# Fewer weight chunks in layer 1 on a shorter row ring, and matmuls that keep TensorE busy at both ends

## What is computed

```python
def peer_ffn(h, w_query, sub_keys, expert_u, expert_v):
...
        q = (xb @ w_query).reshape(PEER_BLOCK, PEER_HEADS, 2, D_HALF)
        s = jnp.einsum('thpd,hpkd->thpk', q.astype(jnp.float32), sub_keys.astype(jnp.float32))
        sv, si = lax.top_k(s, TOPK_HALF)
...
        idx = i1 * N_KEYS + i2
        g = jax.nn.softmax(cv, axis=-1)
        u_sel = expert_u[idx]
        a = jax.nn.gelu(jnp.einsum('thkd,td->thk', u_sel, xb))
        return jnp.einsum('thk,thkd->td', g.astype(a.dtype) * a, expert_v[idx])

def reference(...):
...
    for i in range(DEPTH):
        hp = rms_norm(xp, norm_mix[i])
...
            yp, _ = chunk_mlp_mixer(hp, a_w_in[j], a_ln_g[j], a_ln_b[j], a_w_s[j], a_b_s[j], a_w_out[j])
...
            yp, bp = short_conv_mixer(hp, zero_buf, b_w_in[j], b_conv_w[j], b_w_out[j])
...
        f = peer_ffn(tok, peer_w_query[i], peer_sub_keys[i], peer_expert_u[i], peer_expert_v[i])
```

## Time and profile before

| | |
|---|---|
| median of 3 runs | 1724.96 us (1724.49 to 1726.6) |
| the profiled execution, its own time | 1727.62 us |
| its span, first to last instruction | 1725.8 us |
| mean granted TensorE clock | 0.815 |
| TensorE busy | 1316.3 us (76%) |
| VectorE busy | 1086.5 us (63%) |
| ScalarE busy | 651.7 us (38%) |
| GpSimd busy | 632.7 us (37%) |
| moved by DMA | 709.99 MB, 411 GB/s over the span |
| of it by the gathers' queue (q0) | 608.85 MB |

### The profile page before, as it was taken

The page is one execution under the profiler, slowest core; times in us unless marked ns, Lnnn a source line. Parts: engine busy times, 40 slices in busy tenths (PEclk is TensorE's granted clock), DMA queues, the critical chain, the costliest instruction groups (busy, mean ns, idle before and its releaser), DMA issues.

```text
span 1725.8 us, 23657 instructions
## 1 busy us (share of the span) xinstructions
PE 1316.3 (76%) x8378; PEld 631.5 (37%) x8378; DVE 1086.5 (63%) x2681; ACT 651.7 (38%) x2105; POOL 632.7 (37%) x596
## 2 busy tenths in 40 slices
PE   8998988998975678777754688797897667666744
PEld 7993545644540145433100355352462111111100
DVE  1359578555764756565676755767587666666454
ACT  2125444334433432243443423333643434434343
POOL 2014334433442433233344333434444443344341
PEclk9998999998985799997655799798897666667655
DMA  9989999999999999999999999999999999999997
GB/s 379 403 357 415 398 420 422 420 421 421 411 422 421 421 421 420 421 418 421 419 412 421 402 422 421 421 415 416 397 420 411 422 422 421 421 420 419 419 398 306
DMA packets 99382, 709.99 MB, mean 411 GB/s; under 512 B 11488, under 2 KB 11920, under 8 KB 13600
## 3 DMA queue, kind: packets, MB, share of 16 engines
q0 software_dynamic: 84192, 608.85, 85.4%
q1 hardware_dynamic: 14352, 99.16, 14.0%
q10 hardware_dynamic: 720, 0.48, 0.1%
HBM read 706.92 MB, written 1.52 MB: 410 GB/s over the span
## 4 chain that ended last, share of the span: by engine, by line
DMA 49%; PE 32%; ACT 7%; DVE 7%; issue 3%; POOL 2%; DVEq 0%; ACTq 0%; SPq 0%; POOLq 0%
DMA uvring<-expert_uv_dram,idx 48%; PE psum L841 12%; PE psum L852 11%; DVE uvring L1587 5%; PE psum L905 3%; PE psum L1017 3%; POOL uvring L789 2%; ACT diag L1189 1%; ACT wgt L1185 1%; ACT L1177 1%; ACT a_gelu L1177 1%; PE psum L1039 1%; PE psum L860 1%; PE psum L1000 1%; ACT L1075 1%
## 5 line engine op out<-in xcount | busy, mean ns | idle before, releaser
L1587 DVE SCALAR_TENSOR_TENSOR uvring<-uvring,xn 128x1024 f32<-128x1024 f32 x576 | 705.0, 1225 | 531.0 <-DMA uvring<-expert_uv_dram,idx 525.1
L789 POOL DMA_INDIRECT uvring<-expert_uv_dram,idx x576 | 623.9, 1083 | 1038.7 <-PE psum L841 848.8
L841 PE MATMUL psum<-uvring,diag 64*64 64x512 f32 x4096 | 686.4, 764 | 293.0 <-ACT diag L1189 280.4
L1177 ACT ACTIVATE a_gelu<-a_raw 128x1 f32<-128x1 f32 x576 | 116.6, 202 | 867.2 <-DVE uvring L1587 866.8
L841 PEld LDWEIGHTS psum<-uvring,diag 64*64 64x64 f32 x4096 | 130.7, 154 | 722.9 <-ACT diag L1189 636.6
L1189 ACT ACTIVATE diag<-twin,wgt 128x64 f32<-128x64 f32 x512 | 178.1, 348 | 48.8 <-ACT wgt L1185 1.9
L1185 ACT ACTIVATE wgt<-a_gelu,gate 128x1 f32<-128x1 f32 x576 | 169.5, 294 | 21.1 <-ACT a_gelu L1177 0.4
L833 PE MATMUL psum<-uvring,diag 128*32 128x256 f32 x512 | 67.6, 634 | 94.2 <-ACT diag L1189 83.6
L852 PEld LDWEIGHTS psum<-xT,wring 128*128 128x128 f32 x864 | 118.9, 198 | 42.0 <-issue 41.1
L852 PE MATMUL psum<-xT,wring 128*128 128x160 f32 (+1 forms) x864 | 130.3, 306 | 0.0
L852 PEld LDWEIGHTS psum<-xT,kept 128*128 128x128 f32 x896 | 115.3, 192 | 33.9 <-issue 32.3
(11 more groups left out here) (186 smaller groups left out, 957.3 us busy)
## 6 DMA issues: line engine op xcount, KB each, us to landing
wring<-w_chunks_dram SPq DMA_DIRECT2D x51, 1024.0 KB, 10.1
kept<-w_chunks_dram SPq DMA_DIRECT2D x20, 1024.0 KB, 14.3
uvring<-w_chunks_dram SPq DMA_DIRECT2D x17, 1024.0 KB, 17.3
uvring<-expert_uv_dram,idx POOLq DMA_INDIRECT x576, 13.4
arena<-w_chunks_dram SPq DMA_DIRECT2D x2, 1024.0 KB, 14.4
uvring<-w_chunks_dram SPq DMA_DIRECT2D x2, 512.0 KB, 7.4
uvring<-ln_gain_dram POOLq DMA_DIRECT2D x1, 1024.0 KB, 9.4
uvring<-ln_bias_dram POOLq DMA_DIRECT2D x1, 1024.0 KB, 15.0
```

The costliest lines, as they stand in the source:

```text
L789: pool.indirect_dma_start(uvring[:, n % RING, :], None, expert_uv, bass.IndirectOffsetOnAxis(ap=idx[t][:, i:i + 1], axis=0),).then_inc(uv_ ...
L841: mm = nc.tensor.matmul(acc[64 * j:64 * j + 64, 512 * i:512 * (i + 1)], diag[64 * i:64 * i + 64, n % DIAGS, :], row[64 * i:64 * i + 64, D ...
L1177: nc.scalar.activation(a_gelu[:, c:c + 1], a_raw[:, c:c + 1], ACT.Gelu_apprx_tanh).then_inc(gelu_done, 1)
L1587: nc.vector.scalar_tensor_tensor(out=uvring[:, slot, 0:D], in0=uvring[:, slot, 0:D], scalar=1.0, in1=xn[t][:, :], op0=ALU.mult, op1=ALU.mu ...
```

## The change

**Layer 1 holds 14 chunks.** For its two passes chunks 0 to 11 get a place of their own until the second pass has used them (`HELD`): eight in `kept`, one in "late", one in the ring's third place, and chunks 0 and 1 in row slots 5 and 6. Chunks 12 to 19 pass through the ring's other two places in the first pass (`PASSED`), and 18 and 19 stay there for the second. Chunks 20 to 23 and 12 to 17 are loaded in the second pass into places whose held chunk was used (`AGAIN`). So layer 1 loads 20 chunks for the first pass and 10 for the second.

**Rows on five slots.** Slot 5 takes no row from 140 up to 304, slot 6 none from 141 up to 306 (`AWAY`); rows there go round the other five (`plan_rows`). SP loads chunks 0 and 1 when the last row before them was used, and POOL waits with rows 305 and 307 until the second pass has used these chunks.

**Planner.** A step that needs a chunk passed through the two ring places may come six turns after the step that frees the place at the earliest (`lands`).

**TensorE busy.** Six matmuls on a tile of zeros at the program's start, two on the identity ahead of the first chunk, and three behind each of the four rows before the last. Their results are not used.

**First chunks in parts.** The first chunk is loaded in quarters, one of them by ACT's queue, the second in halves.

```diff
+HELD = {2: ("kept", 1), 3: ("kept", 2), 4: ("kept", 3), 5: ("kept", 4), 6: ("kept", 0), 7: ("late", 0),
+        8: ("kept", 5), 9: ("kept", 6), 10: ("kept", 7), 11: ("ring", 2), 0: ("slot", 5), 1: ("slot", 6)}
+PASSED = {c: ("ring", c % 2) for c in range(12, 20)}
+AGAIN = dict(zip(LATE + list(range(12, 18)), (HELD[c] for c in range(2, 12))))
+
+AWAY = {5: (140, 305), 6: (141, 307)}
...
+    second, third = PASS_CHUNK0[2], PASS_CHUNK0[3]
+    for c, at in [*HELD.items(), *PASSED.items()]:
+        loads.append((at, [second + c] + [third + c] * (c not in AGAIN)))
+    for c, at in AGAIN.items():
+        loads.append((at, [second + c] * (c in LATE) + [third + c]))
...
+def plan_rows():
...
+        s = min((s for s in range(RING) if s not in AWAY or not AWAY[s][0] <= n < AWAY[s][1]),
+                key=lambda s: latest.get(s, s - RING))
...
+            passed = [("lands", ("out", 1, c - 2, 0, 0), 6)] if n == 2 and c >= 2 else []
...
-            for n in range(PASS_CHUNK0[2], PASS_CHUNK0[3]):
-                load_chunk(n)
...
+            for at, users in LOADS[len(first):]:
+                load_chunk(at, users[0])
...
+                if at[0] == "slot" and l == 1:
+
+                    sp.wait_ge(v_tensor, max(m for m in range(AWAY[at[1]][0]) if SLOT[m] == at[1]) + 1)
...
-                if n >= RING:
-
-                    pool.wait_ge(v_tensor, n - RING + 1)
+                if n in ROW_AFTER:
+                    wait_unused(pool, ROW_AFTER[n])
+                if ROW_BEFORE[n] is not None:
+
+                    pool.wait_ge(v_tensor, ROW_BEFORE[n] + 1)
...
+            for q, done in ((1, quarter_landed[1]), (2, quarter_landed[2]), (3, landed)):
+                s = slice(2 * q, 2 * q + 2)
+                sp.dma_start(place[:, s, :], w_chunks[0][:, s, :]).then_inc(done, 16)
+            place, landed = place_of(1)
+            for s, done in ((slice(0, KD // 2), second_landed), (slice(KD // 2, KD), landed)):
+                sp.dma_start(place[:, s, :], w_chunks[1][:, s, :]).then_inc(done, 16)
...
+            act.dma_start(place_of(0)[0][:, 0:2, :], w_chunks[0][:, 0:2, :]).then_inc(quarter_landed[0], 16)
...
+            def keep_busy(tile, count, at):
+
+                for _ in range(count):
+                    nc.tensor.matmul(at, tile[:, :], tile[:, :], start=True, stop=True)
+
+            pe.wait_ge(step, 1)
+            keep_busy(zeros, 6, acc[:, 0:P])
...
+                    if k == ("v", 0, 0):
+                        keep_busy(ident, 2, acc[:, 0:P])
...
+                        if LAST[1, 2] - 4 <= n < LAST[1, 2]:
...
+                            keep_busy(ident, 3, bank(("qsum", 1, 2), P, at=P))
```

More of the change, by code:

```diff
@@ L78, in plan_homes @@
     queries = [("slot", s) for s in (0, 1, 4, 5, 6)]
-    home, uses, counts = [], {}, {"early": 0, "query": 0, "ring": 0}
+    loads, counts = [], {"early": 0, "query": 0, "ring": 0}
     def take(what, of):
@@ L83, in take @@
         return of[(counts[what] - 1) % len(of)]
-    for n in range(PASS_CHUNK0[-1]):
+    for n in range(PASS_CHUNK0[2]):
         c = n - max(p for p in PASS_CHUNK0 if p <= n)
[L87 to L91, removed]
+        if c in KEPT:
+            if n == c:
+                loads.append((("kept", KEPT.index(c)), [c, PASS_CHUNK0[1] + c]))
             continue
-        if c in kept:
-            at = ("kept", kept.index(c)) if kept.index(c) < KEEP else ("late", 0)
-        elif n == PASS_CHUNK0[1]:
+        if n == PASS_CHUNK0[1]:
             at = ("arena", 0)
@@ L102, in plan_homes @@
             at = take("ring", [("ring", r) for r in range(WRING)])
[L103 to L108, removed]
+        loads.append((at, [n]))
+    second, third = PASS_CHUNK0[2], PASS_CHUNK0[3]
[3 more added lines that the diff above has]
+        loads.append((at, [second + c] * (c in LATE) + [third + c]))
+    home, before, last = {}, {}, {}
+    for at, users in loads:
+        count, previous = last.get(at, (0, None))
+        last[at] = count + 1, users[-1]
+        before[users[0]] = previous
+        for n in users:
+            home[n] = at, count + 1
+    return loads, home, before
+LOADS, HOME, BEFORE = plan_homes()
+def plan_rows():
+    slot, count, before, after, latest = [], [], [], {}, {}
+    for n in range(len(ITEMS)):
+        s = min((s for s in range(RING) if s not in AWAY or not AWAY[s][0] <= n < AWAY[s][1]),
+                key=lambda s: latest.get(s, s - RING))
+        rows = [m for m in range(n) if slot[m] == s]
+        chunks = [users[-1] for at, users in LOADS if at == ("slot", s) and (users[0] >= PASS_CHUNK0[2]) == bool(rows)]
+        if not rows or s in AWAY and rows[-1] < AWAY[s][0] <= n:
+            after[n] = chunks[-1]
+        slot.append(s)
+        count.append(len(rows) + 1)
+        before.append(rows[-1] if rows else None)
+        latest[s] = n
+    return slot, count, before, after
+SLOT, ROW_COUNT, ROW_BEFORE, ROW_AFTER = plan_rows()
 def scores_of(l, t):
@@ L727, in _ @@
             place, landed = place_of(0)
-            for half, done in ((slice(0, KD // 2), first_landed), (slice(KD // 2, KD), landed)):
-                sp.dma_start(place[:, half, :], w_chunks[0][:, half, :]).then_inc(done, 16)
-            for n in range(1, PASS_CHUNK0[2]):
-                load_chunk(n)
+            for q, done in ((1, quarter_landed[1]), (2, quarter_landed[2]), (3, landed)):
[4 more added lines that the diff above has]
+                sp.dma_start(place[:, s, :], w_chunks[1][:, s, :]).then_inc(done, 16)
+            first = [(at, users[0]) for at, users in LOADS if users[0] < PASS_CHUNK0[2]]
+            for at, n in first[2:]:
+                load_chunk(at, n)
                 if 18 <= n < 20:
@@ L807, in chunk @@
                 place, landed = place_of(m)
[L808 to L814 removed]
+                pe.wait_ge(landed, 16 * HOME[m][1])
                 return place
```

88 lines of the change are left out of this document (38 added, 50 removed).

## The result

The change takes 1730.15 us (median of 7 runs, 1727.44 to 1735.85) where the kernel before takes 1724.49 beside it: 1.0036 of its time, 95% interval 1.0025 to 1.0047. It is slower by 5.7 us; 5.7 less were forecast, and the range ended at 1727.5. The profiled execution of the change took 1728.23 us (span 1726.4).

A forecast was written before the change was run, and what follows sets the result against it. DMA transfers set the pace, with holes only in the head and at the end. Bytes -12.4, five slots +10.1, second pass +0.5, head -3.3, tail -0.6 sum to -5.7 on the median 1724.96: 1719.3 us, range 1710 to 1727.5.

The forecast's parts named there:

- the price of the five slots: Rows 140 to 304: holes in the DMA's work from five slots instead of seven, 10.1 us (ends 2 and 22).
- 6.94: Transit of a row from issue at 133.31 to ready at 140.25, leaving 0.9 us to spare on five slots.
- quiet stretch: Rows on five slots: delays beyond the 0.9 to spare now and then, estimated to cost 1.2 us (0 to 3).
- dense part: First pass, some 40 turns: TensorE queues and holds reach 7.7 us with no chunks queued; costs 3 us.
- tile change at row 256: Its matmuls wait for the tile before's sums: hold 7.94, an excess of 2.4 us.
- tile change at row 288 and the start of the second pass: Same shape as at row 256, followed by layer 1's second pass with TensorE full; given 3.5 us.
- Rival 3: Five slots: rows starve because transit beside other traffic is 7.7; price 22, time 1731; chance 0.13.
- Rival 1: Five slots: the transit is short, 5.3, so the price is 2 us in all and the time 1711; chance 0.15.
- Bytes: Layer 1's second pass loads 10 chunks instead of 15, 86 loads instead of 91, saving 12.4 us.
- The head's 3.3: First chunks: filled idle time and quarters let TensorE start and run sooner, saving 3.3 us (1 to 5.7).
- The end of the second pass: Layer 1: nothing left to load from turn 345 on while TensorE is full, adding 0.5 us (0 to 2).
- The tail: Last row's matmuls run at the fast clock level, saving 0.6 us (0 to 0.7).

The follow-up runs named there:

- layer 1 alone: The change without its lines on the first chunks and the extra matmuls: 1731.56 us against 1725.40 for the kernel before, ratio 1.0037.
- six slots: The change with rows 140 to 304 on six slots, chunks 1 and 18 loaded through the ring for each pass: 1718.43 us against 1725.40, ratio 0.9961.
- the longer holds on seven: The kernel before, with ScalarE writing the diagonal three (rows 226 to 254) or six times more (266 to 285): 1733.18 us against 1724.94, ratio 1.0045.
- the runs on three and four slots: Pieces of one run: the change with five groups of rows narrowed to one, two, three or four slots; 1830.71 us in all.
- the first experiment: The kernel before with only the change's lines on the first chunks and the extra matmuls: 1724.33 us against 1725.40, ratio 0.9996.

## Why the prediction was wrong

**The step that failed is the price of the five slots, by its rule "A hold over 12.43 - 6.94 = 5.5 us leaves the DMA engines idle for the excess": its term for the transit was too small.** The rule takes one transit, 6.94. In the change the rows that follow the one before at full pace take 7.6 us or more from issue to landing (55 of 58 such rows between 580 and 700 and between 800 and 878 us; the other three took 7.05 to 7.53). So five slots leave 12.43 - 4.58 - 7.7 = 0.15 us to spare in an ordinary circle and not 0.9, and a hold costs from about 4.7 on and not from 5.5. The change's quiet stretch shows both sides of that edge (window, then timeline):

```profile
820.00:845.00 25.00, 15.72 (x80) 2.95 (x80) 17.66 (x35) 11.37 (x36) 11.56 (x11) 0.70 0.97 379
845.00:870.00 25.00, 16.92 (x80) 2.84 (x80) 16.69 (x51) 7.64 (x28) 8.44 (x9) 0.64 1.01 423
```

```profile
822.32 0.94 POOL L829 DMA_INDIRECT uvring<-expert_uv_dram,idx  x1 [1.55 <-PE psum L875]
...
827.64 1.23 DVE L1634 SCALAR_TENSOR_TENSOR uvring<-uvring,xn 128x1024 f32<-128x1024 f32 x1 [0.60 <-DMA uvring<-expert_uv_dram,idx]
...
829.90 1.28 ACT L1215 ACT_TABLE_LOAD   x1
830.10 1.23 DVE L1634 SCALAR_TENSOR_TENSOR uvring<-uvring,xn 128x1024 f32<-128x1024 f32 x1 [1.23 <-DMA uvring<-expert_uv_dram,idx]
...
836.32 1.92 POOL L829 DMA_INDIRECT uvring<-expert_uv_dram,idx  x1 [3.04 <-PE psum L875]
...
839.99 1.23 DVE L1634 SCALAR_TENSOR_TENSOR uvring<-uvring,xn 128x1024 f32<-128x1024 f32 x1 [1.22 <-DMA uvring<-expert_uv_dram,idx]
...
846.33 1.23 DVE L1634 SCALAR_TENSOR_TENSOR uvring<-uvring,xn 128x1024 f32<-128x1024 f32 x1 [1.99 <-DMA uvring<-expert_uv_dram,idx]
```

The row issued at 822.32 starts its dot at 830.10, 7.78 later and 2.46 behind the row before: five slots keep the full pace here, and from 845 to 870 us they move 423 GB/s. But at 829.90 ScalarE loads a table for the routing, which takes 1.28 us, and then a second one, so this row's weight comes late. The next issue into its slot follows at 836.32, 6.2 us after the landing, and then two rows take 6.34 us (839.99 to 846.33) instead of 4.97.

The same holds over many rows (landings by their semaphores in the trace; "late" is the spacing beyond 2.49). Between 580 and 700 us 43 rows land in the change. The 24 of them that were issued at most 4.8 us after their slot's last row had landed are 0.5 us late together, the other 19 are 7.7. In the run with layer 1 alone it is 24 rows with 0.5 and 18 with 6.9. So the price is paid behind late rows and not in every circle; the spare was too small for so many of them. The medians of issue to landing in the windows hide this, as rows at full pace that stand in a queue take longer too: 404 GB/s at 8.3 us in the change, 411 to 413 at 9.7 to 11.7 on six slots and with the longer holds on seven, 419 at 12.8 before.

The trace of before could have told. The last dot of the earlier trace rows, at 140.25, has no wait before it, so DVE came to it from other work, and 6.94 need not be the landing of that row; and 2.68 was no longer full pace. DVE did wait for the row behind it, which took 8.05 and came 2.60 later:

```profile
134.80 0.94 POOL L789 DMA_INDIRECT uvring<-expert_uv_dram,idx  x1 [0.30 <-issue]
```
```profile
142.85 1.22 DVE L1587 SCALAR_TENSOR_TENSOR uvring<-uvring,xn 128x1024 f32<-128x1024 f32 x1 [0.28 <-DMA uvring<-expert_uv_dram,idx]
```

Term by term, lost time against before from the four stretches: dense part (575 to 700 us) 7.4 against the 3 forecast; quiet stretch (700 to 875, which begins with the pass's output part) 5.0 against 1.2; tile change at row 256 (875 to 900) 2.7 against 2.4; tile change at row 288 and the start of the second pass (900 to 1025) 5.3 against 3.5. The tile change whose hold was read from the trace was near; the dense part and the quiet stretch, whose price hangs on the small spare, were not.

**Rival 3 came true**: price 22 and 1731 forecast, 20.4 and 1730.15 measured, and by the condition it named: 7.7 us beside other traffic, a spare of 0.15, and every hold over 4.7 makes a hole. It had a chance of 0.13, because "that 6.94 itself, in heavier traffic" spoke against it; that row does not, since it was not at full pace. Rival 1 had the transit of a lone row right (5.3; measured 5.5) and the time wrong. The Trainium skill ("DMA: Bandwidth & Descriptors", "Anatomy of one DMA") gives 4.4 for such a row as an estimate; the lone row's 5.5 is nearer to it than 6.94 is. The sum that the prediction drew from it, 1709, supposes that a short transit means a full rate, and the runs on three and four slots deny that.

**What held.** Bytes: 86 loads and 704.77 MB, so -12.4 at 421 GB/s. The sums with it close within 0.6 us of the medians for three kernels (the change, layer 1 alone, six slots); against the profiled executions, from which their rows come, they are 1.7 to 5.3 too high. The head's 3.3 at the second chunk was reached in three of six executions, but only 2.0 of it at the first row (there the condition that the later chunks "must have landed" decided a part of it); by rows this term is about half the forecast size. By time, head and tail alone gave 0.7 by the ratio (2.2 less to 0.9 more), so the 2.1 that the rows give the two ends stand at the edge of what the runs confirm. The end of the second pass (0.5) did not show: 1225 to 1250 us runs at 419 GB/s in the change, against 405. The tail gave 0.5 of 0.6 by rows.

**What to look at was partly wrong too.** The prediction would have read the price from a DMA share under 1.0. The share is 1.00 in the stretch that loses most; the rate shows it.

## What to carry to other kernels

The test for a ring of buffers, circle against hold plus transit, was right here; the transit has to be taken from rows that follow each other at full pace. Here a gather of 1 MB alone took 5.5 us and rows at full pace some 7.7, about three on the way (7.7 / 2.49). Ask then how much is left for a late row, not for an ordinary one: with holds of some 4 us five slots left next to nothing and cost 20 us, six left one row's time, 2.5 us, more and cost 3.6. Before giving buffers to something else, run the old kernel with those buffers left empty: that one run (+14.1 us) would have shown that 12.4 us of saved bytes could not pay for them.

## What the runs showed of the hardware

The share of busy DMA engines is no measure of what they move: 0.99 at 369 GB/s, 1.00 at 395, 1.01 at 420. A lone gather is busy for 1.25 us before its full rate. That this start lies under the bulk of the row before when rows are queued, and is laid bare when they are not, would fit the need for three rows on the way; it is argued from one kind of slice, and no run separated it from unevenness between the 16 engines. Why a row takes 7.7 us at full pace where one alone takes 5.5 stays open.

The clock at the first chunk did not follow from the extra matmuls alone: with the same instructions ahead of them its 16 records took 3.69 us in the first experiment's profile (some 225 ns a record, the 2.4 GHz level) and 5.38 in the change's. The granted clock over the first 25 us is 1.00 and 0.93; alone it can't tell, as it is 1.00 before too, where these records took 408 ns.
